# A diffusion layer's expert routing on one Trainium2 core: keys from ranks on VectorE alone, the gathered queries in another buffer, and the first one-hot groups placed beside the last gathered queries

## The reference, cut to what matters

```python
def peer(h, w_pq, sub_keys, expert_u, expert_v):
    t = h.reshape(-1, D)
    qh = (t @ w_pq).reshape(T, PEER_HEADS, 2, D_HALF)
    scores = jnp.einsum('thpd,hpkd->thpk', qh, sub_keys)          # 128 keys in each of 2 halves
    s_top, i_top = lax.top_k(scores, PEER_TOPK)                   # 16 best keys of each half
    cand = s_top[:, :, 0, :, None] + s_top[:, :, 1, None, :]
    cand_idx = i_top[:, :, 0, :, None] * N_KEYS + i_top[:, :, 1, None, :]
    best, pos = lax.top_k(cand.reshape(T, PEER_HEADS, -1), PEER_TOPK)   # 16 best pairs
    idx = jnp.take_along_axis(cand_idx.reshape(T, PEER_HEADS, -1), pos, axis=-1)
    gate = jax.nn.softmax(best, axis=-1)
    # then, for all 8 heads x 16 experts of a token:
    act = gelu(einsum('td,thkd->thk', tb, expert_u[ib]))
    out = einsum('thk,thkd->td', gb * act, expert_v[ib])
```

## Time and profile before

| | us |
|---|---|
| runs of the kernel, median (lowest, highest) | 3804.49 (3802.6, 3814.27) |
| the profiled execution, its own time | 3810.19 |
| span of the profiled execution | 3808.4 |
| PE busy in the span | 3605.1 (95%) |
| DVE busy | 2660.4 (70%) |
| POOL busy | 1897.4 (50%) |
| ACT busy | 624.6 (16%) |
| layer 0: choices ready to the dense loop's first matmul | 601.80 to 720.08 |
| layer 1: the same | 2461.22 to 2582.29 |

### The profile page before, as it was taken

The page is one execution under the profiler, slowest core; times in us unless marked ns, Lnnn a source line. Parts: engine busy times, 40 slices in busy tenths (PEclk is TensorE's granted clock), DMA queues, the critical chain, the costliest instruction groups (busy, mean ns, idle before and its releaser), DMA issues.

```text
span 3808.4 us, 45352 instructions
## 1 busy us (share of the span) xinstructions
PE 3605.1 (95%) x15346; PEld 2485.7 (65%) x15346; DVE 2660.4 (70%) x5705; ACT 624.6 (16%) x1532; POOL 1897.4 (50%) x1593
## 2 busy tenths in 40 slices
PE   7998997899999999999989999879999999999998
PEld 3445576667666766666755456776776667766666
DVE  4424598887878667666665256888878777677667
ACT  3212216510000000000021121281000000000000
POOL 0011029866676566666502100597566755666663
PEclk9999999999999999999999999999999999999999
DMA  9711206999999999999941121199999999999997
GB/s 396 292 58 52 100 25 112 277 386 401 403 408 408 357 408 400 408 408 408 382 183 39 37 74 70 40 161 365 381 403 405 399 388 379 408 403 408 408 408 282
DMA packets 496520, 1116.54 MB, mean 293 GB/s; under 512 B 201360, under 2 KB 240400, under 8 KB 495104
## 3 DMA queue, kind: packets, MB, share of 16 engines
q0 software_dynamic: 175104, 637.61, 42.4%
q1 hardware_dynamic: 316768, 463.63, 35.3%
q10 hardware_dynamic: 4512, 13.76, 1.0%
HBM read 1068.68 MB, written 46.12 MB: 293 GB/s over the span
## 4 chain that ended last, share of the span: by engine, by line
PE 33%; DMA 11%; POOL 3%; issue 1%; SPq 1%; DVE 1%; ACT 0%; DVEq 0%; ACTq 0%; POOLq 0%
DMA y_nat<-in_peer_ut 11%; PE ps L1494 10%; PE ps L1507 6%; PE ps L580 4%; PE ps L1502 4%; POOL big L2080 3%; PE ps L1427 2%; PE ps L709 2%; PE ps L560 2%; PE ps L1452 1%; SPq L1322 0%; PE ps L1485 0%; PE ps L1440 0%; PE ps L680 0%; PE ps L546 0%
## 5 line engine op out<-in xcount | busy, mean ns | idle before, releaser
L1494 PE MATMUL ps<-big,y_nat 128*128 128x336 f32 x4096 | 1217.6, 451 | 58.1 <-DMA y_nat<-in_peer_ut 51.2
L1494 PEld LDWEIGHTS ps<-big,y_nat 128*128 128x128 f32 x4096 | 762.5, 190 | 441.5 <-issue 102.5
L2095 POOL DMA_INDIRECT big<-in_peer_u,gates_area x608 | 772.3, 1270 | 463.1 <-DVE kn_area L1881 288.7
L2106 POOL DMA_INDIRECT big<-in_peer_v,gates_area x608 | 689.0, 1133 | 415.8 <-DVE big L1899 269.1
L1899 DVE SCALAR_TENSOR_TENSOR big<-big,kn_area 128x1024 f32<-128x1024 f32 x608 | 785.8, 1292 | 7.0 <-DVE big L1899 0.5
L1881 DVE CUSTOM_DVE_ANT_0 big<-big,y_nat 128x1024 f32<-128x1024 f32 x608 | 740.3, 1224 | 1.3
L1609 ACT ACTIVATE gates_area<-ps 128x336 f32<-128x336 f32 x256 | 115.5, 451 | 2038.0 <-PE ps L1494 2038.0
L1507 PEld LDWEIGHTS ps<-gates_area,big 128*128 128x128 f32 x2048 | 363.7, 190 | 61.2 <-issue 61.2
L1507 PEld LDWEIGHTS ps<-gates_area,y_nat 128*128 128x128 f32 x2048 | 363.7, 190 | 61.2 <-issue 61.2
L1507 PE MATMUL ps<-gates_area,big 128*128 128x208 f32 x2048 | 381.0, 339 | 0.0
L1507 PE MATMUL ps<-gates_area,y_nat 128*128 128x208 f32 x2048 | 381.0, 339 | 0.0
(11 more groups left out here) (294 smaller groups left out, 3384.2 us busy)
## 6 DMA issues: line engine op xcount, KB each, us to landing
y_nat<-in_peer_ut SPq DMA_DIRECT2D x256, 512.0 KB, 8.6
y_nat<-in_peer_v SPq DMA_DIRECT2D x128, 512.0 KB, 6.7
big<-in_peer_v SPq DMA_DIRECT2D x128, 512.0 KB, 6.7
big<-in_w_mod SPq DMA_DIRECT2D x24, 2048.0 KB, 14.2
expert_gates<-big SPq DMA_DIRECT2D x8, 4096.0 KB, 22.2
gates_area<-expert_gates SPq DMA_DIRECT2D x128, 136.0 KB, 9.5
kn_area<-expert_gates SPq DMA_DIRECT2D x128, 136.0 KB, 9.9
big<-in_w_in SPq DMA_DIRECT2D x8, 2048.0 KB, 15.5
```

Source lines behind the costliest of these rows:

```text
L1494: last = pe.matmul(ps[:, 6 + par, 0:NX], u_s[par][:, k, :], h_t[:, k, X0:ND], start=(k == 0), stop=(k == KD - 1))
L2095: pool.indirect_dma_start(out=u_ring[:, k % USLOTS, :], out_offset=None, in_=io["peer_u"][:, :], in_offset=bass.IndirectOffsetOnAxis(ap=ro ...
L2106: pool.indirect_dma_start(out=v_ring[:, k % VSLOTS, :], out_offset=None, in_=io["peer_v"][:, :], in_offset=bass.IndirectOffsetOnAxis(ap=ro ...
```

## The change

Four things are changed.

- **Keys from ranks.** `compare`, `resolve` and POOL's `keys_of_ranks` go, with their two semaphores. `dense_keys` takes their place, for all three tiles at once: one DVE instruction a rank r, (rank == r) x key r, over 24 x 16 slots, written at a stride of 8 elements. After 8 ranks a sum over those 8, after 16 the second sum, and an addition of both. It is called once for the first keys and once for the second, with `softmax` between the two calls.
- **Gathered queries in another room.** They go to `q_g` in `kn_area`, which isn't shared with the one-hots. The waits of DVE and POOL for `s_s` at 4 x PH go.
- **`choices(0)` moves forward** in PE's queue, from behind the last gathered score to ahead of the gathered queries of half 13 (`CHOICE_AT`), into bank 4. The waits for `s_top` and `s_rk` move with it. The groups now use the PSUM pairs 1 and 2 in place of 0 and 1.
- **ACT's order.** The exponential moves from behind all gathered work to half 5. The copy of tile 0's choices stands behind half 13's query and half 12's score, and the scaling of the groups 0, 1 and 2 behind the halves 14, 15 and 16. The groups 0 and 1 are evacuated together ahead of the scaling of group 3. The 128 x 2048 copy `sc_4` moves from ahead of the exponential to behind the scaling of group 6.

```diff
+CHOICE_AT, CHOICE_BANK = 13, (4, 6, 7)
-        q_r = carve(big, 21504, 2, ND)
+        q_r, q_g = carve(big, 21504, 2, ND), carve(kn_area, 2048, 2, len(GATHERED) * P)
-        eq_a = y_nat[:, 0:3, :]
+        eq_a, key_tail = y_nat[:, 0:3, :], carve(gates_area, 4 * T, DENSE, P)
...
 (TensorE)
+                    def choices(i):
+                        if i == 0:
+                            pe.wait_ge(s_top, PH)
+                            pe.wait_ge(s_rk, 1)
+                        else:
+                            pe.wait_ge(s_sbe, 2 * PH)
...
                     for g in range(2 * PH + 1):
+                        if g == CHOICE_AT:
+                            choices(0)
...
-                    pe.wait_ge(s_top, PH)
-                    pe.wait_ge(s_sbe, 2 * PH)
-                    pe.wait_ge(s_rk, 1)
-                    choices(0)
...
 (ScalarE)
+                        if g == 5:
+                            act.wait_ge(s_b7, 1)
+                            act.activation(exp_gate[:, 0:DENSE, :], gate_xa, ACT.Exp).then_inc(s_e7, 1)
+                        if g == CHOICE_AT:
+                            choices(0)
+                        if g >= 2 * PH + 1 - HOTS:
+                            scale_hots(g - (2 * PH + 1 - HOTS))
+                    for n in range(HOTS, GROUPS):
...
+                        if n == HOTS:
+                            evacuate(0)
+                            evacuate(1)
+                        scale_hots(n)
+                        if n == HOTS + 3:
+                            act.activation(sc_4, sc_b[:, 0, :, :]..., ACT.Copy).then_inc(s_sbe, 1)
+                        evacuate(n - 1)
...
 (VectorE)
-                    for u in range(4 * DENSE):
-                        compare(u, eq_a, (rowf_a, colf_a))
-                        if u >= 2:
-                            resolve(u - 2, u - 1, 0, eq_a)
...
+                    def dense_keys(x, rank, dst):
+                        eq = eq_a.rearrange("p t d -> p (t d)").rearrange("p (s k a) -> p s k a", k=TOPK, a=TOPK // 2)
+                        key = top_ifa.rearrange("p t (h x) a -> p (t h) x a", x=2)
+                        for half in range(2):
+                            for a in range(TOPK // 2):
+                                r = half * TOPK // 2 + a
+                                lane.do(dve.scalar_tensor_tensor(
+                                    out=eq[:, :, :, a], in0=rank.rearrange("p t (h k) -> p (t h) k", k=TOPK), scalar=float(r),
+                                    in1=key[:, :, x, r:r + 1].broadcast_to([P, DENSE * PH, TOPK]), op0=ALU.is_equal, op1=ALU.mult))
+                            lane.settle()
+                            lane.do(dve.tensor_reduce((dst, key_tail)[half].rearrange("p t s -> p (t s)"),
+                                                      eq.rearrange("p s k a -> p (s k) a"), AX.X, ALU.add))
+                            lane.settle()
+                        lane.do(dve.tensor_tensor(dst, dst, key_tail, ALU.add))
+                    dense_keys(0, rowf_a, exp_i1[:, 0:DENSE, :])
                     softmax(0, DENSE, 1)
+                    dense_keys(1, colf_a, exp_i2[:, 0:DENSE, :])
...
-                    dve.wait_ge(s_s, 4 * PH)
...
 (GpSimd)
-                    for u in range(4 * DENSE):
-                        keys_of_ranks(u, u + 1, eq_a, top_ifa)
-                    pool.wait_ge(s_s, 4 * PH)
```

74 lines of the change are left out of this document (24 added, 50 removed).

## The result

The changed kernel is slower: 3827.28 us (median of 4 runs, 3823.13 to 3829.37) against 3803.63 us for the kernel before (4 runs). The ratio is 1.006, with a 95% interval of 1.0047 to 1.0072, that is 18 to 27 us. The forecast was 3789.5, and the range ended at 3801. The profiled execution took 3828.13 us against 3810.19.

The account below looks back on a forecast made before the run. PE mostly ends last, then expert-block DMA; POOL's one-hots pace the gates. A layer wins 13.4 - 6.2 - 0.5 = 6.7 us; two layers plus 1.5 give 14.9, rounded 15.0: 3804.5 - 15.0 = 3789.5 us, range 3780 to 3801.

Parts of the forecast that it names:

- term 1: DVE's new key products and sums: products 0.475 us apart, stride free, so choices are ready 13.4 us earlier a layer.
- term 3: ACT's evacuations up to group 9 and SP's first store: two near ties, together costing 0.5 us a layer.
- The first rival: DVE's strided products cost twice, 0.875 us each: 12 us slower, 3816.5 us; decides against from 0.68 us; chance 0.06.
- The rule: SBUF's 16-byte lines: where fewer than two accesses hit a line, crossing pays, so every write of dense_keys would pay.
- Term 2: Handover from choices ready to POOL's group 4: PE idles 5.6 us, its clock drops; 6.2 us a layer given back.
- Term 4: Layer 1's second drop of PE's clock, near group 5: may be escaped; half counted, 1.5 us won, once.

Follow-up runs that it names:

- the cheap layout: The changed kernel with products writing every second element instead of every eighth, the sum adding over two axes; 3808.19 us, ratio 1.0012 to the kernel before.
- run with choices last: The changed kernel with choices(0) and the scaling of groups 0 to 2 behind the last gathered score again; 3807.29 us, ratio 0.9994 to the kernel before.
- run with filler: The changed kernel with two unread 128 x 128 PE products ahead of every group from group 3 on; 3813.92 us, ratio 1.0029 to the kernel before.
- run with six POOL rows: The changed kernel with POOL making 6 one-hot rows in four groups instead of 7, DVE one more; 3824.9 us, ratio 1.0056 to the kernel before.

## Why the prediction was wrong, point by point

Two steps failed, one in term 1 and one in term 3.

**Term 1, the products: mis-sized.** The first step that failed is "the two points, 64 elements in 0.135 and 384 in 0.47 us, lie on about 1.05 ns an element plus 0.07 us, so the stride costs nothing there". One of the two points had the stride and the other had not, and the one with the stride was too short to show it: eight of 64 elements take 1.21 us with it and 1.17 without. The measured value is 0.70 us. From the first product to choices ready it took 39.80 us (596.16 less 556.36) and 32.23 with the cheap layout (588.19 less 555.96), so the stride's price is 7.6 us a layer. Instead of 13.4, choices were ready 5.6 us earlier in layer 0 (the products also began 0.5 us later than in the compares' place, at 556.36). The rest of the term held: sums 3.35 us, no wait for the exponential, and with the cheap layout 588.19 us instead of 588.4.

**The first rival** had the right mechanism at too high a price (0.875 us), and a chance of 0.06. Its point of decision, 0.68 us a product, was right: with the measured price the sum becomes 15.0 - 2 x 7.6 = -0.2 us, no change. That is about what is measured where the slow groups are mostly gone (ratios 1.0003 and 1.0001, with one and three of the nine left).

**The rule.** The row showed no cost at 64 bytes of stride, and I went by the row. The measured products pay 0.23 us at 16 bytes and beyond, and nothing at 8. The Trainium skill, page "SBUF — State Buffer", section "Specifications (TRN2)", with its lines of 16 bytes that want two accesses each, names exactly this edge; where two elements share a line nothing is paid. It gives no size: the measured factor is 5.76 to 3.84 us, 1.5, not 2.

**Term 2, the handover: right.** Expected were 5.6 us of PE standing with choices at 588.4; choices came 7.8 us later than that, and it stood 12.89. Choices were copied 7.9 us after ready (603.59 + 0.48 - 596.16; 7.6 forecast), PE's groups 0 and 1 started right behind the last score, and group 9 was evacuated 41.4 us after ready (637.56 - 596.16; 41 forecast). The granted clock did fall, to 0.50 from 588 on, and half 13's queries took 5.84 us instead of 3.62. From choices ready to group 9's start it was 31.63 us before (633.43 less 601.80) and 38.33 after (634.49 less 596.16): 6.7 us given back, 6.2 forecast. The run with choices last shows that this price was one of the place, and that the place was not forced.

**Term 3, ACT and the stores: the second step that failed.** "Both are near ties, together 0.5 us a layer. Ends: 0 and 3 us." Behind it stands "the end of the gates is therefore fixed by when POOL can begin group 4": the term follows ACT and POOL up to group 9 and gives nothing behind it a price. I looked at `sc_4` as a delay of ACT's own queue up to group 9, and there it was a near tie. The stores were no matter: the first was issued at 625.35, 13.5 us after the last score, as forecast, and their landing took 22.1 us in the median (22.2). What I did not follow was the delay's effect on the other engines behind group 9. I had treated POOL's row as fixed at 1.54 us, when it is a mean of rows of 0.79 and of about 2 us, whose mix depends on gaps in DVE's work. Four groups then take 13.17 us (652.40 less 639.23) instead of 10.50, so a slow group costs some 2.65 us, and nine of them 24 us. The whole row says the same: from group 9's start to the dense loop it was 86.65 us before (720.08 less 633.43) and 99.13 after (733.62 less 634.49), 12.5 us more, and 12.4 us more in layer 1.

**Term 4.** Layer 1's slow group of the kernel before, at groups 4 and 5, did not come: group 9 started 37.9 us after choices ready, about as in layer 0. But four others came behind group 9.

**The sum, with what was measured.** 15.0 won as forecast, less 15.2 for the stride, less 24 for the slow groups is 24.2 slower; measured are 18 to 27 us. The sum is a check of sizes only, since the forecast's 15 had the one slow group of layer 1 half in it. In layer 0 the parts close: choices 5.6 us earlier, 6.7 given back, 12.5 lost behind group 9, together 13.5 later. Of my rivals none had the second loss. The one that ended on the slow side, at 3816.5, had 12.8 us a layer for the stride where 7.6 were measured, and nothing for the slow groups. That it lies nearest to the result is in part luck.

**What is shown, and what isn't.** Shown by runs: the stride's price, alone and within the kernel; that the copy's place sets off most of the slow groups, in both kernels; that fewer rows for POOL do not cure them. That the lower clock makes them longer is read from pairs of rows with the same idle stretch (3.81 against 5.43 us behind 2.72), and the run with filler fits it. That VectorE's unbroken work makes POOL's rows long, and that the pattern goes on because each slow group lets DVE run ahead again, is read from the traces too; no run varied either alone. Why the row recovers by itself after some of them, as in layer 0 behind 696.33, was not tried.

## What to carry to other kernels

A cost per element that is read from a short instruction is no cost for a long one: look for a row of the same length, or put both ends of the stride in the range. An engine's even pace beside a neighbour is not its own speed; before delaying anything in a balanced row of four engines, look at single instructions for what that pace is made of. And when work is moved forward, put the wait where the data will be ready by the trace, and keep each delay (here 1.9 us of ACT) at the start of the row, where everyone is waiting anyway.

## What the runs showed of the hardware

- VectorE products in float32 of 384 elements: 0.47 us from start to start where writes are 4 or 8 bytes apart, 0.70 where they are 16 or 32. A sum over 3072 elements takes 3.35 us reading them in order (row 562.14 above) and 5.38 reading at a distance of 384 elements; read as pairs from four blocks, 3.35.
- A GpSimd row of 128 elements takes 0.79 us by itself. It takes about 2.3 to 2.5 us if it begins just after VectorE has started its two comparisons with two inputs (POOL at 634.2 and 636.7, DVE at 634.13 and 636.58). In the kernel before, VectorE has gaps of 0.19 us, and short rows begin there:

```profile
L2080 POOL TENSOR_SCALAR big<-iota_k,gates_area x1: 787/787/787, 642.9 to 642.9; 128x128 f32<-128x128 f32 x1
```

```profile
642.24 0.74 DVE L1860 TENSOR_SCALAR big<-iota_k,gates_area 128x128 f32<-128x128 f32 x2
643.17 0.83 DVE L1852 TENSOR_TENSOR big<-iota_k,gates_area 128x640 f32<-128x640 f32 x1 [0.19 <-PE ps L1485]
```

A gap of 0.19 us on VectorE thus goes with a row of 0.79 us in place of one of 2.0 to 2.5; no run varied the gap by itself. The Trainium skill, page "GPSIMD Engine Reference", section "1. Specifications", says that the two share their SBUF interfaces and contend where a VectorE instruction has two SBUF inputs; L1852 and L1855 have two, and the traces agree.
- PE's granted clock fell after stretches without a matmul of about 2.7 us in the gates (0.70 from 640 to 644, 0.58 from 652 to 656), and stayed at 1.00 behind one of 2.27 us (638.89 in the run with filler), though it fell behind another of 2.27 (0.60 from 652 to 656). It also stayed at 1.00 behind 2.72 us (636.03 in the kernel before with the copy in group 6) and behind 2.95 us (703.94 in the run with six POOL rows, where the pair took 3.81 us). So the length of the stretch alone does not say whether the clock falls.
